# Conditioning projections with the weight tiles stationary, and input squares summed on TensorE

## The reference, cut to what matters

```python
mod   = silu(c) @ w_mod + b_mod            # (1024) @ (1024, 6*1024)
sh1, sc1, g1, sh2, sc2, g2 = split(mod, 6)
mod_c = silu(c_ctx) @ w_mod + b_mod        # only its sh1 and sc1 are used
h_lat = rms_norm(x_lat, norm1_g) * (1 + sc1) + sh1
h_ctx = rms_norm(x_ctx, norm1_g) * (1 + csc1) + csh1
y     = hgrn2_mixer(h_lat, h_ctx, ...)     # 8 heads, projections of h, a gated scan
x_lat = x_lat + g1 * y
h2    = rms_norm(x_lat, norm2_g) * (1 + sc2) + sh2
x_lat = x_lat + g2 * moe_ffn(h2)           # 16 experts
```

## Time and profile before

| | us |
|---|---|
| median of 3 runs | 3500.41 (3500.4 to 3500.5) |
| the profiled execution | 3500.34 |
| its span, first to last instruction | 3498.6 |
| granted TensorE clock, mean over the span | 0.948 of full |

### The profile page before, as it was taken

How to read it: one execution, slowest core, us unless ns; L and a number is a source line. 1 busy time by engine, 2 the same in 40 slices (tenths; PEclk the granted TensorE clock), 3 DMA queues, 4 the chain that set the end, 5 groups by cost and what they waited for, 6 DMA issues and landing times.

```text
span 3498.6 us, 44912 instructions
## 1 busy us (share of the span) xinstructions
PE 3161.8 (90%) x16582; PEld 2569.9 (73%) x16582; DVE 1877.3 (54%) x2579; ACT 1386.3 (40%) x1905; POOL 177.7 (5%) x169
## 2 busy tenths in 40 slices
PE   5988888578996999899888999999998999889997
PEld 4777777467875888666776888878887778678886
DVE  6554555367985444678536544563446333464435
ACT  4445544446774222446314322342224332343222
POOL 0000000000001000143100000010001000010000
PEclk8999989699998999999998999999999999999999
DMA  4311111138992322221001222323232222123322
GB/s 170 127 55 59 67 56 52 42 123 337 392 352 78 97 95 96 86 70 61 23 2 61 96 96 96 104 83 97 95 96 96 71 74 91 50 71 102 98 97 76
DMA packets 98049, 357.66 MB, mean 102 GB/s; under 512 B 11008, under 2 KB 11392, under 8 KB 97536
## 3 DMA queue, kind: packets, MB, share of 16 engines
q1 hardware_dynamic: 92448, 334.54, 28.1%
q0 software_dynamic: 4176, 15.24, 1.2%
q10 hardware_dynamic: 1296, 6.11, 0.5%
HBM read 344.29 MB, written 11.56 MB: 102 GB/s over the span
## 4 chain that ended last, share of the span: by engine, by line
PE 75%; DVE 11%; ACT 8%; issue 4%; DMA 1%; POOL 0%; ACTq 0%; DVEq 0%; POOLq 0%
PE bank L281 19%; PE bank L282 18%; PE bank L283 18%; DVE x L496 2%; PE bank L1631 1%; PE bank L1633 1%; PE bank L1632 1%; PE gbank L929 1%; ACT whi L259 1%; PE bank L2612 1%; DVE h_lo_buf L450 1%; ACT h_hi_buf L439 1%; ACT L352 1%; DVE cum L1075 1%; PE gbank L911 1%
## 5 line engine op out<-in xcount | busy, mean ns | idle before, releaser
L281 PE MATMUL bank<-h_hi_buf,whi 128*128 128x512 f32 x2320 | 931.2, 401 | 55.6 <-DVE h_lo_buf L450 35.7
L282 PE MATMUL bank<-h_lo_buf,whi 128*128 128x512 f32 x2320 | 912.7, 393 | 0.0
L283 PE MATMUL bank<-h_hi_buf,wlo 128*128 128x512 f32 x2320 | 911.8, 393 | 0.0
L259 ACT ACTIVATE whi<-raw 128x1024 fp32r<-128x1024 f32 x466 | 477.2, 1049 | 433.3 <-PE bank L283 379.0
L272 DVE TENSOR_TENSOR wlo<-raw,whi 128x1024 fp32r<-128x1024 f32 x444 | 533.5, 1221 | 138.5 <-ACT whi L259 71.8
L281 PEld LDWEIGHTS bank<-h_hi_buf,whi 128*128 128x128 f32 x2320 | 442.7, 191 | 173.7 <-DVE h_lo_buf L450 49.0
L282 PEld LDWEIGHTS bank<-h_lo_buf,whi 128*128 128x128 f32 x2320 | 442.5, 191 | 94.6 <-issue 5.0
L283 PEld LDWEIGHTS bank<-h_hi_buf,wlo 128*128 128x128 f32 x2320 | 441.2, 190 | 94.4
L281 PE MATMUL bank<-a_hi_buf,whi 128*128 128x512 f32 x960 | 377.1, 393 | 25.0 <-DVE a_lo_buf L3193 9.6
L282 PE MATMUL bank<-a_lo_buf,whi 128*128 128x512 f32 x960 | 376.0, 392 | 0.0
L283 PE MATMUL bank<-a_hi_buf,wlo 128*128 128x512 f32 x960 | 375.7, 391 | 0.0
(11 more groups left out here) (514 smaller groups left out, 3899.4 us busy)
## 6 DMA issues: line engine op xcount, KB each, us to landing
raw<-in_w SPq DMA_DIRECT2D x634, 512.0 KB, 3.4
x<-in_x ACTq DMA_DIRECT2D x2, 2048.0 KB, 10.9
sorted_rows<-zrow POOLq DMA_DIRECT2D x7, 514.0 KB, 8.4
xrow<-sorted_rows POOLq DMA_DIRECT2D x7, 514.0 KB, 6.7
sorted_y<-ysb POOLq DMA_DIRECT2D x7, 512.0 KB, 7.4
out<-x SPq DMA_DIRECT2D x8, 256.0 KB, 2.0
xc<-in_xc ACTq DMA_DIRECT2D x1, 1024.0 KB, 8.5
waup<-in_waup ACTq DMA_DIRECT2D x1, 256.0 KB, 4.9
```

What stands on the lines that cost most here:

```text
L259: act.activation(k.whi[:, g.slot, :], k.raw[:, g.slot, :], ACT.Copy).then_inc(k.split_hi, 1)
L281: pe.matmul(out, w_hi, hi, start=(t == 0), stop=False)
L282: pe.matmul(out, w_hi, lo, start=False, stop=False)
L283: return pe.matmul(out, w_lo, hi, start=False, stop=(t == tiles - 1))
```

## The change

`Mod` and all later conditioning blocks swap the operands. For each 128 x 128 weight tile the tile is the stationary operand; the moving one holds four columns, hi and lo of `c` and `c_ctx` side by side (`c_parts`), and for the lo weights two. A block is 16 matmuls with 16 weight loads, for both vectors at once; it has its own four columns of a bank, and counts as done by itself. VectorE only adds hi and lo parts, with one small reduction for a group of blocks.

The squares move into `Mod`: from the fifth block on ScalarE squares one chunk behind each split, latent chunks first, and TensorE multiplies it with ones as it is (fp32), accumulating over the eight chunks; VectorE's additions go. Both Ln and then both Exp stand together. VectorE multiplies each input chunk by the root in place; ScalarE makes hi from that, with gain and shift, while VectorE makes the full `h` and then lo: three VectorE instructions for a chunk where there were two. The latent chunks go first, the context follows; the first head's context product waits for each of its chunks (`ready_more`). The lower bounds' sums and reciprocals come last.

At the start ScalarE issues `c`, then the latent input, the context, and the vectors last; `Mod` waits for `c` alone. The halving moves to `HgrnOutput`, whose loops over blocks are written out. The rest of the diff renames semaphores.

```diff
-def pe_mod(k, slot, blocks, tiles, out, which):
+def pe_mod(k, slot, out):
     pe = k.nc.tensor
-    width = blocks * P
-    hi = k.whi[:, slot:slot + blocks, :].rearrange("p s f -> p (s f)")
-    lo = k.wlo[:, slot:slot + blocks, :].rearrange("p s f -> p (s f)")
-    for t in tiles:
-        c_hi = k.c_hi[:, t, which:which + 1].to_broadcast([P, P])
-        c_lo = k.c_lo[:, t, which:which + 1].to_broadcast([P, P])
-        w_hi, w_lo = hi[:, t * width:(t + 1) * width], lo[:, t * width:(t + 1) * width]
-        pe.matmul(out, c_hi, w_hi, start=(t == 0), stop=False)
-        pe.matmul(out, c_lo, w_hi, start=False, stop=False)
-        last = pe.matmul(out, c_hi, w_lo, start=False, stop=(t == DC - 1))
+    for t in range(DC):
+        w_hi, w_lo = k.whi[:, slot, t * P:(t + 1) * P], k.wlo[:, slot, t * P:(t + 1) * P]
+        c_both, c_hi = k.c_parts[:, t, :, :].rearrange("p r w -> p (r w)"), k.c_parts[:, t, 0, :]
+        if t < DC - 1:
+            pe.matmul(out, w_hi, c_both, start=(t == 0), stop=False)
+            pe.matmul(out[:, 0:2], w_lo, c_hi, start=False, stop=False)
+        else:
+            pe.matmul(out[:, 0:2], w_lo, c_hi, start=False, stop=False)
+            last = pe.matmul(out, w_hi, c_both, start=False, stop=True)
     return last
...
+    k.nc.vector.tensor_reduce(dst, bank[:, 0:4 * blocks].rearrange("p (b r w) -> p b w r", r=2, w=2), AX.X, ALU.add
+                              ).then_inc(k.bank_free, blocks)
...
 class Mod(Phase):
+    AHEAD = 4
...
     def pe(self, k, q):
+        for g in range(self.blocks):
+            pe.wait_ge(k.split_lo, g + 1)
+            pe_mod(k, g % RING, mod_out(k.bank[g // RING], g % RING)).then_inc(k.block_done, 1)
+            if g >= self.AHEAD:
+                HgrnInput.pe_square(k, q, g - self.AHEAD)
+        for n in range(self.blocks - self.AHEAD, 2 * DC):
+            HgrnInput.pe_square(k, q, n)
...
     def act(self, k, q):
+        for g in range(self.blocks):
+            act_split(k, At(g))
+            if g >= self.AHEAD:
+                HgrnInput.act_square(k, g - self.AHEAD)
+        for n in range(self.blocks - self.AHEAD, 2 * DC):
+            HgrnInput.act_square(k, n)
+        for g in range(self.blocks, self.blocks + LEAD):
             act_split(k, At(g))
...
 class Hgrn(Phase):
...
-            pe_mod(k, 1, MOD_BLOCKS, range(DC), k.bank[1][:, 0:MOD_BLOCKS * P], 0).then_inc(k.block_done, MOD_BLOCKS)
+            for b in range(MOD_BLOCKS):
+                wait(pe, k.split_lo, g + b + 2)
+                pe_mod(k, 1 + b, mod_out(k.bank[1], b)).then_inc(k.block_done, 1)
...
 class HgrnInput(Phase):
+    def pe_square(k, q, n):
+        pe = k.nc.tensor
+        wait(pe, k.sq1_ready, n + 1)
+        out = HgrnInput.sums(k, n)
+        pe.matmul(out, k.ones[:, :], k.sq1[:, n % 2, 0:out.shape[-1]], start=(n % DC == 0), stop=(n % DC == DC - 1)
+                  ).then_inc(k.norm_sum if n % DC == DC - 1 else k.sq1_added, 1)
...
     def dve(self, k, q):
+        scaled(0)
+        scaled(1)
+        for n in range(2 * DC):
+            c, w = n % DC, n // DC
+            width = T if w == 0 else TC
+            h32 = k.h321[:, n % 2, 0:width]
+            wait(dve, k.x_scaled, n + 1)
+            dve.tensor_scalar(h32, self.source(k, n), k.gain1[:, w, c:c + 1], k.shift1[:, w, c:c + 1], ALU.mult, ALU.add
+                              ).then_inc(k.h_made, 1)
+            if n + 2 < 2 * DC:
+                scaled(n + 2)
+            wait(dve, k.h_made, q.h + n + 1)
+            wait(dve, k.h_hi, q.h + n + 1)
+            hi, lo = (k.h_hi_buf[:, c, :], k.h_lo_buf[:, c, :]) if w == 0 else (k.hc_hi[:, c, :], k.hc_lo[:, c, :])
+            dve.tensor_tensor(lo, h32, hi.bitcast(F32), ALU.subtract).then_inc(k.h_ready, 1)
```

More of the change, by code:

```diff
@@ L757, in dve @@
         dve.wait_ge(k.c_ready, 2)
-        dve.tensor_tensor(k.c_lo[:, :, :], k.c32[:, :, :], k.c_hi[:, :, :].bitcast(F32), ALU.subtract).then_inc(k.c_ready, 1)
-        for g in range(LEAD):
+        dve.tensor_tensor(k.c_parts[:, :, 1, :], k.c32[:, :, :], k.c_parts[:, :, 0, :].bitcast(F32), ALU.subtract
+                          ).then_inc(k.c_ready, 1)
+        for g in range(self.blocks + LEAD):
             dve_split(k, At(g))
[L761 to L767, removed]
+            if g % RING == 1 and g > 1:
+                n = g // RING - 1
+                dve.wait_ge(k.block_done, RING * (n + 1))
+                dve_mod(k, k.bank[n], RING, RING * n)
 HEADS = 8
@@ L1162, in advance @@
     def advance(self, q):
-        q.sq += 2 * DC
         q.norm += 2
@@ L1196, in pe, with source, act_square @@
     def pe(self, k, q):
-        pe_norm(k, q.norm, q.sq + DC, TC)
-        pe_norm(k, q.norm + 1, q.sq + 2 * DC)
+        pass
+    @staticmethod
+    def source(k, n):
+        return k.x1[:, n, :] if n < DC else k.xc1[:, n - DC, :]
+    @staticmethod
+    def act_square(k, n):
+        act = k.nc.scalar
+        src = HgrnInput.source(k, n)
+        wait(act, k.x_loaded if n < DC else k.xc_loaded, 16)
+        if n == DC + 1:
+            wait(act, k.norm_sum, 1)
+        else:
+            wait(act, k.sq1_added, n - 1 if n <= DC else n - 2)
+        act.activation(k.sq1[:, n % 2, 0:src.shape[-1]], src, ACT.Square).then_inc(k.sq1_ready, 1)
@@ new lines, in sums, with act_roots @@
+    @staticmethod
+    def sums(k, n):
+        return k.nbank[:, :] if n < DC else k.cbank[:, 0:TC]
+    @staticmethod
+    def pe_square(k, q, n):
[4 more added lines that the diff above has]
+                  ).then_inc(k.norm_sum if n % DC == DC - 1 else k.sq1_added, 1)
+    @staticmethod
+    def act_roots(k, q):
+        act = k.nc.scalar
+        for n in range(2):
+            wait(act, k.norm_sum, q.norm + n + 1)
+            out = (k.lnv[:, :], k.silg[:, 0:TC])[n]
+            act.activation(out, HgrnInput.sums(k, DC * n), ACT.Ln, bias=k.eps_col[:, :], scale=1.0 / D).then_inc(k.ln_ready, 1)
+        for n in range(2):
+            wait(act, k.ln_ready, q.norm + n + 1)
+            src, out = ((k.lnv[:, :], k.rstd[:, :]), (k.silg[:, 0:TC], k.osq[:, 0:TC]))[n]
+            act.activation(out, src, ACT.Exp, scale=-0.5).then_inc(k.rstd_ready, 1)
@@ L1209, in act @@
[L1209 to L1213 removed]
+        for n in range(2 * DC):
+            c, w = n % DC, n // DC
+            wait(act, k.x_scaled, n + 1)
+            wait(act, k.mod1, 6)
+            hi = k.h_hi_buf[:, c, :] if w == 0 else k.hc_hi[:, c, :]
+            act.activation(hi, self.source(k, n), ACT.Identity, bias=k.shift1[:, w, c:c + 1],
+                           scale=k.gain1[:, w, c:c + 1]).then_inc(k.h_hi, 1)
```

180 lines of the change are left out of this document (71 added, 109 removed).

## The result

The changed kernel took 3508.1 us at the median of 8 runs (3504.3 to 3522.4), the kernel before 3498.13 of 8 (3494.3 to 3500.5): the ratio is 1.0039, with an interval of 1.0027 to 1.0051. It is 10 us slower where 29 were forecast. The eight runs lie in two groups, five at 3504.3 to 3508.5 and three at 3519.3 to 3522.4, so the median depends on how many fall in each; their mean is 13.4 us above that of the kernel before. Taken again in later rounds (12 runs against 29 of before) the median was 3512.67 against 3497.71, 15 us, ratio 1.0037 (1.0023 to 1.0052), and the means were 13.6 us apart. The direction was right, the size about twice to three times too large, and the time lies inside the range.

What follows compares the result with a forecast made beforehand. TensorE, busy for 90% of the span, was taken as the bound where it is the late engine. Prologue 16.8, seven heads 10.5 and router 2 sum to 29 on 3500.34: 3529 us, range 3503 to 3546.

Steps and rivals of the forecast that it cites:

- Start: Kernel start: `Mod` waits for `c` alone, so the first matmul comes at 8.7 us, 2.7 us sooner.
- sixteen blocks: `Mod`'s conditioning blocks: half clock throughout, 3.42 us each for 2.78 before; with the squares they end at 83.9 us.
- roots: Square roots behind `Mod`: latent root at 89.0 us, 1.1 us later than before although one pair of tables is saved.
- `h`: VectorE's passes behind the latent root: 1.65 us a latent chunk for 1.45 before; TensorE ends the first product at 112.1.
- head 0's group: First head's 48 conditioning matmuls: start at the half clock and take 10.3 us, to 122.4.
- the mark: Start of the matmul behind the first head's conditioning blocks, 107.60 us before the change: forecast 14.8 us late.
- The first rival: In `Mod`, unpaused small matmuls reach 2.4 GHz in the fifth block: 3479 us in all, faster; chance 0.12.
- The third rival: Weight loads of fp32r tiles don't slow with the clock: `Mod` at 57 us, about 3500 in all, no change; chance 0.06.
- Seven other heads: Conditioning blocks of the later heads: longer group and clock fall cost 4.8 us, less slack: 1.5 a head, 10.5 in all.
- Router: Router's first conditioning group grows from some 7 to 13.7 us, partly hidden: +2 us, bounds -1 and +4.
- The second rival: Heads cost nothing, as the clock may fall behind each short group, inside the slack: 3518 us; chance 0.17.

## Why the prediction was right in its sign and wrong in its size

**Start, sixteen blocks, roots, `h`, head 0's group: right.** The first matmul was forecast at 8.7 and came at 8.57; a block took 3.42 us as forecast; `Mod` ended at 85.0 for 83.9; the latent root was done at 90.2 for 89.0 and the first projection stood at 93.37 for 92.0; the group began at 112.7 for 112.1 and took 10.1 for 10.3; the mark was 15.2 us late where 14.8 were forecast. The input's 2 MB ahead of the weight blocks were costed at nothing, and ScalarE waited 2.23, 3.32 and 1.13 us for three blocks, but TensorE only 0.60. Three VectorE passes take 1.66 us a chunk as forecast. Small errors cancel: the roots are 1.2 us late, since the last square's buffer came free at 83.56 for 82.2, and the way from the first projection to the group took 19.3 us for 20.1.

**The first rival, steady small matmuls lift the clock, is refuted**: 75 us of them, with no pause but 0.60 us, left it at the half level, and 256 columns under the same loads lifted it at 12.6. From 16 to 50 us TensorE was busy for 33.87 of 34.00 us in the one and 33.88 in the other, with starts 0.213 and 0.111 apart. So these two runs show what the prediction read from two stretches: here weight loads in a row did not lift the clock, and columns did. **The third rival, loads that don't slow down with the clock, is refuted too**: with fp32r tiles they stood 0.213 us apart at the half and 0.111 at the full clock.

**The step that failed is "Seven other heads", with its 1.5 us each and 10.5 in all.** The two exchanges of the heads' form were worth +0.9 and +0.3 us by their medians, -0.8 and -0.8 by their means. The stretch from the mark to the last `osq` sum, in the two profiles with the old form in the heads and the eight with four columns:

| us | old form | new form |
|---|---|---|
| mark to head 1's `v_st` | 54.0, 54.0 | 59.3 to 60.6 |
| head 1's to head 7's `v_st`, six turns | 421.4, 419.9 | 411.6 to 424.7, mean 418.9 |
| head 7's to the last head's | 62.6, 63.6 | 60.0 to 61.6 |
| from there to the last `osq` sum | 33.1, 28.0 | 27.7 to 33.4 |
| in all | 571.1, 565.4 | 560.8 to 573.1, mean 568.6 |

So the forecast's cost is there, but once: up to head 1's `v_st` the new form takes 5.4 to 6.7 us more, where the sum had 3.5 (the 2 us of cold dense work behind head 0's group and 1.5 for head 1). On this way the old form never leaves the full clock, and the new one does:

```profile
107.60:161.56 53.96, 53.70 (x257) 45.30 (x256) 29.40 (x45) 23.93 (x28) 3.91 (x7) 1.00 0.49 165
```

```profile
122.81:182.15 59.34, 59.34 (x282) 50.10 (x283) 28.93 (x44) 22.03 (x26) 3.90 (x7) 0.92 0.41 142
```

The six turns behind it cost nothing more, 0.3 us less each in the mean, and the end gives back about 4: in all 568.6 against 568.3, with only two profiles of the old form to compare.

A later turn shows why. The fall inside the group was there as forecast:

```profile
442.80 0.25 PE L702 MATMUL bank<-c_parts,wlo 128*128 128x2 f32 x1
442.91 0.27 PE L704 MATMUL bank<-c_parts,wlo 128*128 128x2 f32 x1
443.05 0.35 PE L705 MATMUL bank<-c_parts,whi 128*128 128x4 f32 x1
443.26 0.35 PE L701 MATMUL bank<-c_parts,whi 128*128 128x4 f32 x1
...
446.67 0.78 PE L281 MATMUL bank<-h_hi_buf,whi 128*128 128x512 f32 x1
...
461.96 0.82 PE L899 MATMUL gbank<-ident,v_st 128*128 128x128 f32 x6
```

The group takes 7.0 us, z backward begins at the half clock, and the wait in front of `v_st` is gone, as said. What the sum had too small is what comes back behind `v_st`. The kernel before, in the same head, has the waits, and its small matmuls behind `v_st` at 0.62 of the clock:

```profile
409.66 1.12 PE L951 MATMUL nbank<-osq,ones 128*128 128x512 f32 x2 [1.52 <-ACT osq L1028]
...
424.28 0.50 PE L281 MATMUL bank<-h_hi_buf,whi 128*128 128x512 f32 x1 [0.63 <-DVE wlo L272]
...
440.01 0.87 PE L904 MATMUL gbank<-ident,v_st 128*128 128x128 f32 x6 [1.75 <-DVE kk L1100]
```

```profile
369.30:378.30 9.00, 7.35 (x35) 5.96 (x35) 2.29 (x3) 5.27 (x11) 0.00 (x0) 0.62 0.16 58
```

The changed kernel has the same work at the full clock, 7.0 us instead of 9.0:

```profile
392.00:399.00 7.00, 4.59 (x34) 3.57 (x33) 1.17 (x2) 5.18 (x11) 0.00 (x0) 1.00 0.19 75
...
430.41 1.12 PE L946 MATMUL nbank<-osq,ones 128*128 128x512 f32 x2 [1.52 <-ACT osq L1023]
```

From `osq` to the next `v_st` it is 31.55 us (461.96 - 430.41) against 30.35 before: +1.2. From a `v_st` to the `osq` behind it, 38.35 (430.41 - 392.06) against 40.37: -2.0. The forecast had +2.4 and -0.9: it charged the group twice what it costs here and put what is spared behind `v_st` at less than half. Both turns have a granted clock of 0.93 in the mean; only the place of the fall differs. With the wait for `kk` TensorE used to rest 1.75 us and lose the clock on the small matmuls behind; without that rest it keeps it there. All profiles agree: in heads 1 to 7 with four columns there was no rest ahead of `v_st`, and the clock of the 9 us behind it was 1.00 in all 56 cases; with a rest of 1.3 to 1.8 us, in 23 cases of the old form and of 128 columns, it was 0.62 to 0.69. (Shorter rests, in five other heads of those forms, went with 0.81 or 1.00.) How long a head spends at the half clock varies within one profile, and the turn's length goes with it; two turns of the changed kernel:

```profile
320.54:392.06 71.52, 64.10 (x345) 55.21 (x344) 35.83 (x67) 35.00 (x57) 0.00 (x0) 0.90 0.17 59
...
461.96:530.28 68.32, 60.90 (x346) 52.66 (x345) 35.74 (x67) 35.00 (x57) 0.00 (x0) 0.95 0.18 61
```

The changed kernel's heads lasted 68.3, about 70 or 71.5 us, those before 67.1 to 72.0. The spread is that of the place where the falls come, and it is as large as the effect that was to be forecast.

**"Router", +2, was worth nothing.** From the last `osq` sum to `member` it is 88.2 us after (774.73 - 686.56) and 88.3 before, though the way from the first group's start to the router's matmul grew from 8.9 to 14.3 us; that is inside the bounds of -1 to +4.

**The second rival**, heads that are free since the clock falls behind the group, came nearer with its 3518, but for another reason: the clock does fall inside the group.

**The sum with the measured terms**: 15 for the prologue, about 0 for heads and router, against 13.4 and 13.6 measured by the means. The 3.8 us between `member` and the end in the first profile (2727.9 against 2731.7) are no effect that can be claimed: the second profile of the same program has 2729.1, and the other nine, whose code differs there by one hidden group at most, have 2729.4 to 2733.1. What stays open is why the runs of the changed kernel and of some variants fall into groups some 12 to 16 us apart. Of the 12.2 us that the way from the first projection to the mark grew by, 5.9 are head 0's group at the half clock; that the other 6.3 are VectorE's third pass and the order of the chunks is read from the traces, and a version with the old two passes wasn't tried.

## What to carry to other kernels

Here a matmul with its own 128-column weights cost its load, 0.21 us at the half clock and 0.11 at the full, with 4 fp32r columns as with 256, so those columns were free, and their use was not only arithmetic: a stream of loads with hardly a column left this TensorE at half its clock for 75 us, and idle columns bought 34 us back. Look for the clock in the distance of two starts, not in the busy share. In a loop that has a wait and a fall of the clock in each turn, a saving or a cost ahead of the wait is no sum by itself: follow it through the whole turn, look at the turns apart that had no such wait, and measure over many runs, because where the fall lands moves the time by more than such a term. Where runs lie in two groups, compare means as well as medians.

## What was unexpected of the hardware

Repeating four columns 64 times is free even at the full clock: 0.111 us a matmul, as with four (442.80 to 442.91). The changed kernel spreads over 3498.4 to 3522.4 in 20 runs, and most of its variants as widely (3484.9 to 3503.1 with the old `Mod`, 3491.0 to 3513.3 with fp32r squares), where the kernel before stays in 3490.3 to 3504.3 over 65. The kernel that holds the full clock through each head's group was the slower one, 3520.1 against 3508.1 and 3512.7; the small matmuls behind `v_st` then ran at 0.64, as they do in the old form, and the way from head 7's `v_st` to the last head's took 63.8 us against 60.0. And a clock figure of 1.00 ahead of the first recorded change is not a reading.
